# Gathered expert rows of the context tokens: pick places cast once, eight row buffers, an unrolled GpSimd program and another queue order in the value stage of a two-layer step

## What is computed

```
sc = einsum(q, subkeys); sv, si = top_k(sc, 16)          # 8 heads x 2 sides x 128 keys
best, ci = top_k(sums of pairs, 16); idx = i1 * 128 + i2 # 8 x 16 = 128 picks per token
gsm = softmax(best)
act = gelu(einsum('td,thkd->thk', xb, u_tab[idx]))
out = einsum('thk,thkd->td', gsm * act, v_tab[idx])       # 16384 experts, rows of 1024
```

## Time and profile before

| what | us |
|---|---|
| median of the runs | 5015.15 |
| the profiled execution | 5005.07 |
| its span, first to last instruction | 5003.3 |
| TensorE busy (matmuls) | 4526.0, 90% |
| VectorE busy | 3145.1, 63% |
| GpSimd busy | 2654.9, 53% |
| ScalarE busy | 1177.7, 24% |
| value stage of layer 0, first matmul | 1601.3 |
| value stage of layer 1, first matmul | 4151.9 |

### The profile page before, as it was taken

How to read it: one execution, slowest core, us unless ns; L and a number is a source line. 1 busy time by engine, 2 the same in 40 slices (tenths; PEclk the granted TensorE clock), 3 DMA queues, 4 the chain that set the end, 5 groups by cost and what they waited for, 6 DMA issues and landing times. The chain is left out here.

```text
span 5003.3 us, 77426 instructions
## 1 busy us (share of the span) xinstructions
PE 4526.0 (90%) x27516; PEld 4053.8 (81%) x27516; DVE 3145.1 (63%) x6219; ACT 1177.7 (24%) x1696; POOL 2654.9 (53%) x1462
## 2 busy tenths in 40 slices
PE   7789999999999888888869889999999998999997
PEld 6768999999998666666658679999999997777775
DVE  6962498199994666566643431992799973444444
ACT  2052111132322222222222431110232322222221
POOL 3403455444443777777752124555444436888885
PEclk9889999999999999999988999999999999999998
DMA  5401244377677666666621011444577676666773
GB/s 203 149 9 60 84 120 120 109 154 159 155 162 202 234 244 239 250 236 250 240 76 35 26 47 64 119 119 122 124 159 162 153 172 237 249 251 252 250 253 131
DMA packets 823649, 797.66 MB, mean 159 GB/s; under 512 B 566513, under 2 KB 601041, under 8 KB 822898
## 3 DMA queue, kind: packets, MB, share of 16 engines
q1 hardware_dynamic: 175248, 500.38, 29.8%
q10 hardware_dynamic: 603106, 159.70, 14.8%
q0 software_dynamic: 45056, 134.38, 7.7%
HBM read 640.41 MB, written 153.89 MB: 159 GB/s over the span
## 5 line engine op out<-in xcount | busy, mean ns | idle before, releaser
L498 PE MATMUL acc<-a_hi,w_hi 128*128 128x320 f32 x5296 | 1671.5, 316 | 45.8 <-DVE a_lo L1270 32.3
L500 PE MATMUL acc<-a_hi,w_lo 128*128 128x320 f32 x5296 | 1641.9, 310 | 0.1
L499 PE MATMUL acc<-a_lo,w_hi 128*128 128x320 f32 x5296 | 1641.5, 310 | 0.0
L498 PEld LDWEIGHTS acc<-a_hi,w_hi 128*128 128x128 f32 x5296 | 1000.5, 189 | 51.2 <-issue 35.1
L499 PEld LDWEIGHTS acc<-a_lo,w_hi 128*128 128x128 f32 x5296 | 1001.1, 189 | 1.4 <-issue 0.2
L500 PEld LDWEIGHTS acc<-a_hi,w_lo 128*128 128x128 f32 x5296 | 999.2, 189 | 0.4 <-issue 0.4
L420 POOL TENSOR_TENSOR w_lo<-w_in,w_hi 128x1024 fp32r<-128x1024 f32 (+1 forms) x345 | 891.7, 2585 | 27.7
L436 POOL CAST w_hi<-w_in 128x1024 fp32r<-128x1024 f32 x256 | 306.4, 1197 | 1060.9 <-DMA w_in<-in_u 1060.9
L464 POOL TENSOR_TENSOR w_lo<-w_in,w_hi 128x1024 fp32r<-128x1024 f32 x256 | 698.7, 2729 | 53.8 <-ACT w_hi L1096 49.0
L741 PE MATMUL aux<-p_his,w_hi 128*128 128x512 f32 x1024 | 445.4, 435 | 272.0 <-POOL w_lo L464 149.5
L1505 DVE SCALAR_TENSOR_TENSOR one_b<-iota_b,picks_t 128x384 bf16<-128x384 bf16 x1024 | 633.5, 619 | 0.0
(11 more groups left out here) (244 smaller groups left out, 6265.5 us busy)
## 6 DMA issues: line engine op xcount, KB each, us to landing
w_in<-in_u SPq DMA_DIRECT2D x256, 512.0 KB, 4.0
w_in<-in_v SPq DMA_DIRECT2D x256, 512.0 KB, 5.9
gate_s<-gates ACTq DMA_DIRECT2D x64, 1024.0 KB, 14.0
ag<-act_s SPq DMA_DIRECT2D x256, 256.0 KB, 4.7
ag<-gate_s SPq DMA_DIRECT2D x256, 256.0 KB, 5.3
act_s<-a_out ACTq DMA_DIRECT2D x184, 256.0 KB, 3.6
w_mod_v<-in_w_mod SPq DMA_DIRECT2D x48, 512.0 KB, 3.6
act_s<-tmp ACTq DMA_DIRECT2D x72, 256.0 KB, 3.6
```

Of the source, the lines that this page charges most:

```text
L498: pe.matmul(out, wh, hi[:, k, n], start=(k == 0), stop=False)
L499: pe.matmul(out, wh, lo[:, k, n], start=False, stop=False)
L500: return pe.matmul(out, wl, hi[:, k, n], start=False, stop=(k == kt - 1))
```

## The change

- The places of all 128 picks are cast once, in `route`, into `where_i`; `next_where` goes.
- `found` has eight buffers instead of four, and the activations have a column for each pick (`pick_act`). Pick n's row gather waits for `added` of pick n - 8.
- GpSimd's value program is written out instead of looped: eight row gathers before the first `w_lo`, eight activation gathers at chunk 6, and from chunk 8 on `w_lo`, row, activation of the same chunk number as before.
- SP's loop: `load_ag` stands ahead of `load_values` and waits for `p_lo` (chunk - 4) instead of `p_made`, since the product is now made in place in `ag`.
- ScalarE's loop: `high_p` stands ahead of `high_v`.
- `total`, the buffers of the modulation weights and others get new addresses. ScalarE's exponential of the gates stands one body of the expert stage earlier.

```diff
-SPLIT = 8
+SPLIT, FOUND = 8, 8
...
-        w_mod_v = at("w_mod_v", [P, 3, D], work + 40960)
+        w_mod_v = [at(f"w_mod_v{i}", [P, D], off) for i, off in
+                   enumerate((work + 49152, act_at + 32768, act_at + 36864))]
...
-        found = at("found", [P, 4, D], work + 20480)
+        found = at("found", [P, FOUND, D], work + 16384)
...
                 def load_ag(c, u):
                     if not (isinstance(c, int) and c < 4):
-                        sp.wait_ge(p_made, NKEY * l + c - 3)
+                        sp.wait_ge(p_lo, NKEY * l + c - 3)
...
                 with sp.Fori(1, BODIES) as i:
                     for u in range(SPLIT):
+                        load_ag(u + SPLIT * i, u)
                         sp.wait_ge(v_done, NKEY * l - SPLIT + u + 1 + SPLIT * i)
                         load_values(u + SPLIT * i, u)
-                        load_ag(u + SPLIT * i, u)
...
+            def fetch_row(l, k):
+
+                if PICKS * l + k >= FOUND:
+                    pool.wait_ge(added, PICKS * l + k - FOUND + 1)
+                pool.indirect_dma_start(found[:, k % FOUND, :], None, rows_of_v,
+                                        bass.IndirectOffsetOnAxis(ap=where_i[:, 0, k:k + 1], axis=0))\
+                    .then_inc(found_in[k % FOUND], 16)
...
+            def values_of(l):
+                pool.wait_ge(where_ready, l + 1)
+                for k in range(2):
+                    pool.wait_ge(gates_out[k], 16 * PIECES * 2 * (NT - 1) * (l + 1))
+                for k in range(FOUND):
+                    fetch_row(l, k)
+                for c in range(NKEY):
+                    if c == 6:
+                        for s in range(4):
+                            pool.wait_ge(a_st[s], 32 * A_ALL[s] * (l + 1))
+                        for k in range(FOUND):
+                            fetch_act(l, k)
+                    slot = (VC[l] + c) % SPLIT
+                    pool.wait_ge(hi_v, NKEY * l + c + 1)
+                    pool.tensor_tensor(w_lo[:, slot, :], landing(slot), w_hi[:, slot, :].bitcast(F),
+                                       ALU.subtract).then_inc(lo_done, 1)
+                    if c >= FOUND:
+                        fetch_row(l, c)
+                        fetch_act(l, c)
...
                 with act.Fori(1, BODIES) as i:
                     for u in range(SPLIT):
+                        high_p(i, u)
                         high_v(i, u)
-                        high_p(i, u)
...
-                for half in range(2):
-                    next_where(half, 4 * half)
+                dve.tensor_copy(where_i[:], where[:]).then_inc(where_ready, 1)
```

More of the change, by code:

```diff
@@ L229, in build @@
         hi_v, where_ready = sem("hi_v"), sem("where_ready")
-        found_in = [sem(f"found_in{i}") for i in range(4)]
+        found_in = [sem(f"found_in{i}") for i in range(FOUND)]
         act_in = [sem(f"act_in{i}") for i in range(2)]
@@ L479, in _ @@
                 split_loop(l)
-                for k in range(2):
-                    pool.wait_ge(gates_out[k], 16 * PIECES * 2 * (NT - 1) * (l + 1))
-                values_loop(l)
+                values_of(l)
         @block.tensor
@@ L1104, in high_p @@
                         act.wait_ge(v_done, n - SPLIT + 1)
-                    act.activation(p_his[:, u, :], p_raw[:, u % 2, :], ACT.Copy).then_inc(p_hi, 1)
+                    act.activation(p_his[:, u, :], ag[:, u % 4, 0, :], ACT.Copy).then_inc(p_hi, 1)
                 for c in range(NKEY - SPLIT + BRIDGE, NKEY):
@@ L1525, in low_p @@
                     dve.wait_ge(p_hi, n + 1)
-                    dve.tensor_tensor(p_los[:, k, :], p_raw[:, k % 2, :], p_his[:, k, :].bitcast(F), ALU.subtract)\
+                    dve.tensor_tensor(p_los[:, k, :], ag[:, k % 4, 0, :], p_his[:, k, :].bitcast(F), ALU.subtract)\
                        .then_inc(p_lo, 1)
@@ L1553, in add_row @@
                     u = 4 * half + j
-                    dve.wait_ge(found_in[j], 16 * (QUADS * l + half + 1) + 32 * q)
+                    dve.wait_ge(found_in[u], 16 * (OCTETS * l + 1) + 16 * q)
                     wait(dve, added, k)
                     if first:
-                        dve.tensor_scalar(total[:], found[:, j, :], part_now[:, u:u + 1], None, ALU.mult)\
+                        dve.tensor_scalar(total[:], found[:, u, :], part_now[:, u:u + 1], None, ALU.mult)\
                            .then_inc(added, 1)
                     else:
-                        dve.scalar_tensor_tensor(total[:], found[:, j, :], part_now[:, u:u + 1], total[:],
+                        dve.scalar_tensor_tensor(total[:], found[:, u, :], part_now[:, u:u + 1], total[:],
                                                  ALU.mult, ALU.add).then_inc(added, 1)
@@ L1572, in chunk, with body @@
                     low_p(i, u)
-                def body(i, last=False):
+                def body(i):
                     for u in range(SPLIT):
@@ L1585, in experts @@
                     chunk(0, u, 0, 0, first=True)
-                dve.wait_ge(added, PICKS * l + 4)
-                next_where(0, 8)
-                with dve.Fori(1, BODIES - 1) as i:
+                with dve.Fori(1, BODIES) as i:
                     body(i)
-                body(BODIES - 1, last=True)
                 parts(BODIES - 1, 1)
```

46 lines of the change are left out of this document (22 added, 24 removed).

## The result

The change takes **4842.03 us** (median of 4 runs, 4839.35 to 4844.54) against 5015.34 (4 runs, 5010.95 to 5023.17): a ratio of 0.9653 [0.9636, 0.9669], 173 us less. Its profiled execution took 4839.35 us with a span of 4837.5, which is 165.8 less than the span of before. In it TensorE is busy for 4467.3 us, VectorE for 3287.4, GpSimd for 2570.4 and ScalarE for 1177.3.

A forecast was written before the change was run, and what follows sets the result against it. It took a loop of GpSimd's gathers and VectorE's boundary as the bound. Starts 47, layer 0 58 and layer 1 29 make 134 us off 5005.1: 4871, plus 10.1 to the median, 4881 us; range 4790 to 4970.

The forecast's parts named there:

- the start: Start of each layer's value stage: early rows and `w_lo` finish pick 11 sooner, 24 and 23 us, together 47 us.
- a sign against it: Listed sign that the forecast is wrong: TensorE waits for `p_los` instead of `w_lo`; no size given.
- layer 0: Steady quads of layer 0: 4.0 us gained per body, 58 us in all, bounds 7 and 101.
- the first half of a body: Layer 0's boundary at a body's head: 1.4 us from earlier `w_lo` plus 1.0 us from SP's spread loads.
- From T to P: From a quad's last activation gather's end (T) to its waiting `part_now` (P): 5.4 us in layer 0's first half, 1.0 regained.
- the 2.67 us: GpSimd's idle wait at a layer 1 boundary for a row buffer, claimed to be what the new buffers free.
- ScalarE's order "takes part of it back": Boundary: `w_hi` queues behind `p_his`, so next chunk's `w_lo` starts 4.73 us after `part_now` instead of 6.12, 1.39 earlier.
- The buffers lengthen no lookahead: Value stages: pick n is still gathered in chunk n, and VectorE still needs four activations at each boundary.
- A: Rival: collisions of GpSimd and VectorE fade, layer 1 becomes TensorE's; 238 us gained, 4777 us; chance 0.16.
- B: Rival: collisions eat the steady gain, only the starts stay; 4964 us; chance 0.20.
- C: Rival: GpSimd loses the port for a whole VectorE burst, `w_lo` 4.6 us later; slower, 5101 us; chance 0.10.
- D: Rival: nothing moves, another wait of the boundary takes the place; 5015 us; chance 0.04.

The follow-up runs named there:

- experiment 9: The change without its head start: pick c is gathered in chunk c from 0 on, behind the wait for the activation stores; 4879.94 us.
- experiment 3: The change with SP's loop alone turned back, `load_ag` behind `load_values`; 4853.94 us.
- experiment 6: The kernel before with only the places cast once and GpSimd's value program written out, four buffers and old queue orders kept; 4955.54 us.
- (7): The change with four row buffers instead of eight and ScalarE's loop turned back to values first; 4902.05 us.
- experiment 1: The change with ScalarE's loop alone turned back, `high_v` ahead of `high_p`; 4737.36 us.
- experiment 10: The kernel before with eight row buffers and what makes room for them; GpSimd's loop, late start and old ScalarE and SP orders kept; 4781.55 us.
- experiment 5: The change with every pick gathered four chunks sooner, same buffers and row waits; 4675.60 us.
- experiment 2: The change with four row buffers instead of eight, four rows and activations gathered ahead; 4885.54 us.
- experiment 4: The change with VectorE's additions of gathered rows cut from 1024 to 64 columns; 4697.16 us.

## Why the prediction was right, point by point

**Size and sign** came out, 4842 for 4881 and inside the range, and most of its steps are there to be seen: the start (23.3 and 24.6 us for 24 and 23), `w_lo` of n+1 waiting for `w_hi` at P+4.64 (P+4.73), quads of layer 1 at 24.02 us (24.17), pick 11 done 44.8 us after the first activation (42 to 46). Of the start's 48 us the head start itself is 34 (experiment 9); the sum took it for all of them. TensorE does wait for `p_los` now, which the prediction had named as a sign against it. In layer 0 it did so before the change too, which the prediction, reading for both layers, did not see; the sign alone doesn't decide, as the quads of layer 1 got shorter by what was forecast.

**The mis-sized term is layer 0**: 83.5 us for 58, within its bounds (7 to 101). It was the first half of a body that was taken too low. There two things improved, at the boundary where the prediction counted 1.4 us and 1.0 us for SP's loads. From T to P the mean went from 5.77 to 4.38 us, of which experiment 3 shows 0.80 to be SP's order. And `w_lo` of n+2 no longer comes late, a gain that the sum does not have:

```profile
2061.63 2.88 POOL L470 TENSOR_TENSOR w_lo<-w_in,w_hi 128x1024 fp32r<-128x1024 f32 x1 [3.29 <-ACT w_hi L1096]
2064.67 1.77 POOL L446 DMA_INDIRECT found<-in_v,where_i  x1 [0.15 <-issue]
2066.74 0.94 POOL L452 DMA_INDIRECT pick_act<-act_p,where_i  x1 [0.30 <-issue]
2067.71 2.55 POOL L470 TENSOR_TENSOR w_lo<-w_in,w_hi 128x1024 fp32r<-128x1024 f32 x1
```

With P at 2056.97, the `w_lo` of n+1 starts at P+4.66 and takes 2.88 us, for 4.9 in 13 of 14 bodies before at this boundary, and that of n+2 starts at P+10.74, for a mean of P+14.6. In the mean over the traces' bodies the first half went from 30.26 to 26.19 us, 4.1 where 2.4 were counted; the second half from 28.27 to 26.51, 1.8 where 1.6 were.

**The step that was incomplete in its cause**, though its number fits, is that what the buffers free is the 2.67 us. In the change they free nothing in the steady state of layer 1 (24.03 us with four rows, 24.02 with eight): with the wait for `w_hi` in place of the row wait, the `w_lo` of n+1 starts at nearly the same instant (P+4.64 for P+4.91). The written-out program, to which the sum gave no term, brings the quad to 24.23 us by itself (experiment 6). It is not shown that only it could: no run has GpSimd's loop, eight buffers and the new order of ScalarE together, and the forecast's step, from the loop, may hold there.

That layer 1 came out so near is in part luck. In the mean over its quads the `w_lo` of n+2 starts at P+10.72 instead of P+13.20, but P comes 3.32 us after T instead of 2.42, and the rest of the quad is 0.4 us longer: 2.5 less 0.9 less 0.4. The prediction reckoned with neither of the two losses and took 1.0 as near the middle of a wide span; 1.15 was measured. Why P comes later was not tried.

**ScalarE's order "takes part of it back"** was right in its mechanism and its instant, but was only used to place `w_lo`, not weighed against leaving the order as it was: the part is 99 us, more than half of the whole gain. A chain of measured kernels adds it up, in per cent of before: written out -1.1 (experiment 6); a start of four, SP's order and product in place -1.2 more (7); eight buffers with their longer start -3.2 more (1); ScalarE's order +2.0 (the change). The sum is -3.5. The shares hold for this order alone: by another, eight buffers in the loop bring -4.7 (10), and the written-out program, the start and SP's order only -0.8 more (1).

**"The buffers lengthen no lookahead"** held: where the same eight buffers are used to gather four chunks ahead, another 164 us go (experiment 5). It does not follow that buffers without lookahead are worth little: with the old order of ScalarE they bring 4.7% (experiment 10).

**The rivals.** A, in which collisions fade, gave 4777 us; 4842 lies between it and the forecast, and collisions did fade in part, in both layers: from before to after, the `w_lo` of n+1 goes from 4.77 to 2.88 us in layer 0's first half and from 3.74 to 2.89 in layer 1, and the boundary's activation gather from 2.22 to 1.21 and from 2.13 to 1.35 (means). B fell with the shorter quads. C fell at the port: `w_lo` of n+1 gets in at P+4.64, and what waits for it is VectorE's add, 3.43 us. Its price was also a little high, as the earlier trace rows end the burst at P+12.2 and not at the P+12.9 that it used. D fell with the whole.

## What to carry to other kernels

Before a wait is removed, look for the one that ends next behind it: the same eight buffers brought 4.7% where the next wait, for `w_hi`, comes a chunk later (experiment 10) and nothing to layer 1's quads where it ended 0.3 us sooner (experiment 2). Count also in which step of the consumer a thing is fetched, and not only how many buffers hold it: with the same buffers, fetching four chunks sooner brought another 3.3% (experiment 5). When an in-order queue gets a new order, ask what the instruction moved forward waits for, since everything behind it now waits for that too; here it tied the weights of a chunk to a product that the slow loop makes. And measure parts in pairs: with two waits in series, taking away either one alone shows little, and the worth of a part depends on the other.

## What was not expected of the hardware

**The gathers' stretch has a simple pattern in the change.** In the rows of GpSimd and VectorE above, the gather at 4337.83 began when the add (4337.69, 1.28 us) had 1.14 us left, and took 1.96 us instead of 0.95; the one at 4345.00 began with 0.92 us left of an add and took 1.76 instead of 0.96; the one at 4347.06, at whose start an add began, took 0.95. Over both layers of the change, all 199 gathers that began with 0.25 to 1.2 us left of a VectorE instruction took 0.95 us plus what was left, less 0.10 to 0.14 us; and the 57 that began with VectorE free and inside which one of its instructions began were not longer (0.94 to 0.96 us, but for one). So in the change a gather waits for VectorE at its own start alone. Row gathers of 128x1024 and activation gathers of 128x1 behave alike.

The pattern leaves out gathers that begin where one VectorE instruction hands over to the next. In the change one of 65 such gathers, which began with 0.06 us left, waited for the next instruction as well. In the kernel before, 58 of 62 did: they began with 0.05 to 0.07 us left and took 2.07 to 3.22 us, as long as if two or three more instructions had been waited for. The 2.09 us of the earlier trace rows and the 3.21 us of the earlier trace rows are of this kind. VectorE around the former, which began at 4307.49:

```profile
4306.27 1.28 DVE L1560 SCALAR_TENSOR_TENSOR total<-found,part_now,total 128x1024 f32<-128x1024 f32 x1
4307.47 0.68 DVE L1526 TENSOR_TENSOR p_los<-p_raw,p_his 128x512 fp32r<-128x512 f32 x1
4308.07 0.68 DVE L1520 TENSOR_TENSOR p_raw<-ag 128x512 f32<-128x512 f32 x1
```

What decides at a hand-over was not tried.

The prediction took it that the Trainium skill, by an inference there, would not have gathers slowed. But the same section ("SBUF — State Buffer", "Who interferes with whom") says that a VectorE instruction with two SBUF inputs contends with a GpSimd instruction that reads SBUF, and a gather reads its places from there: read so, the rule and these rows agree. That it is the reading of the places was not tried by itself.

**A tiny VectorE instruction can cost as much as a large one.** Beside a `w_lo` the 128x4 product took 1.73 us instead of 0.16 (experiment 1; it ended at 4320.61, the `w_lo` at 4320.58), and the 128x64 add 2.43 instead of 0.28 (experiment 4). The Trainium skill ("SBUF — State Buffer", "Who interferes with whom") calls the port pair that VectorE shares with GpSimd an exclusive lock and says that issue order, not the shape of the operation, decides who blocks; both rows agree.

**The same wait ends later in a loop.** Behind the same add a row gather started 0.54 us later in GpSimd's loop than in its written-out program (2.46 and 1.92 us after `part_now`, experiment 6). Which of the loop's instructions takes that time (the register sums, the waits, the semaphore that it counts up) was not tried; nor was a looped program with picks gathered ahead.
